# Moving one PSUM copy ahead of an exponent in the activation engine's order (pooling and state-space decoder trunk)

## The chip, the cores and the metric

The kernel runs on one core of one Trainium2 chip. The metric is the device time in microseconds of one execution. Engines: PE is TensorE, with PEld its weight loads; DVE is VectorE; ACT is ScalarE; POOL is GpSimd; SP is SyncE, which issues the DMAs.

## The reference

Two layers on 512 tokens of width 1024. Layer 0 mixes tokens by causal pooling, layer 1 by a Mamba-2 state-space mixer; each is followed by a squared-ReLU MLP of width 4096. The change lies in the state-space mixer, whose core, per group g of 8 heads and chunk c of 128 tokens, is:

```python
x, dtc, bc, cc = chunks of xs, dt, B, C
xdt = x * dtc[..., None]
a_cs = jnp.cumsum(adt, axis=-1)
seg = a_cs[..., :, None] - a_cs[..., None, :]
decay = jnp.exp(jnp.where(causal, seg, -jnp.inf))
cb = jnp.einsum("bclgn,bcsgn->bcgls", cc, bc)
y_diag = jnp.einsum("bcgls,bcgrls,bcsgrp->bclgrp", cb, decay, xdt)
decay_to_end = jnp.exp(a_cs[..., -1:] - a_cs)
states = jnp.einsum("bclgn,bcgrl,bclgrp->bcgrpn", bc, decay_to_end, xdt)
```

After it the output is gated by SiLU(z), and each group of 512 channels is divided by the root of its mean square (grouped RMSNorm) before the output projection.

## The kernel before, in words

Activations lie with features on partitions and the 512 tokens in the free dimension. Every weight product is done in three matmuls of rounded parts (line 710): a weight tile is rounded by ACT into `w_hi` (line 381), POOL subtracts it from the raw tile into `w_lo` (line 612), and TensorE multiplies high by high, high by low and low by high (lines 712 to 714). A unit is a 128-column slice of weights with 1024 rows, that is eight tiles and 24 matmuls; it is rounded and subtracted in two halves. Two units fit in the buffers, so ACT may round half h of unit u+2 once TensorE is done with half h of unit u (line 379), and POOL follows ACT (line 610). SP loads the raw weights once POOL has subtracted the unit two ahead (line 287).

The state-space mixer runs over groups g = 0 to 3. In each, every engine walks through the same slots t, one unit of the input projection per slot, with the scan's work laid into the slots by hand. All engines execute in the order in which their own loop is written, and semaphores join them. Around the change, in group g:

- TensorE (loop at line 912): after unit t=1 (`T_TOKEN`) `token_major` transposes B into a PSUM bank, `b_misc` (line 861), then takes C by B for all chunks (line 870) and transposes x for chunks 0 to 2 (line 852). After unit t=2 (`T_LATE_TOKEN`) it transposes x of chunk 3 into that same bank, so it waits for `bt_ready`, the copy's semaphore (line 926). After unit t=3, from group 1 on, it waits for the three square sums of the previous group (`ysum`, line 930) and runs `statistic_by_token`, eight recorded matmuls of one column (line 739). Then comes `chunk(g, 0)`: sixteen recorded matmuls of 64 x 128 (line 893), and the state product of the B copy and `decayed` x (lines 906 to 910), which waits for POOL.
- ACT (loop at line 563): each slot rounds one half (`ahead(u, 0)`), does some work, and rounds the other (`ahead(u, 1)`). Slot 1 then has the four squares of the previous group (line 554) and `exp_segments(g, 0)`: eight Relus of 128 x 128 (line 546) and an Exp of 128 x 1024 (line 549). Slot 2 is `ahead(u, 0)`, `b_token(g)` (the copy of the transposed B out of PSUM, line 537), `ahead(u, 1)`, `exp_segments(g, 1)`.
- POOL (loop at line 690): slot 2 is the subtraction of the first half, from group 1 on the three sums of squares (`group_sum`, line 684), the subtraction of the second half, and `decayed` of chunks 0 and 1 (line 671).
- DVE (loop at line 1265): slot 2 is C by B under the mask, x times dt for chunks 0 to 2 (line 1172), the scaling of the unit's output (`gate_in`, line 1245), and `decay_times_cb(g, 0)`, the product of the exponent and the masked C by B (line 1182). Slot 3 begins with x times dt of chunk 3.

The tables that place the work by slot:

```python
CHUNK_AFTER = {3: 0, 5: 1, 7: 2, 9: 3}
FALL_IN = {1: 0, 2: 1, 4: 2, 6: 3}
T_TOKEN, T_LATE_TOKEN = 1, 2
T_STAT, T_SPREAD = 3, 6
```

Of the kernel before, what the change touches and what calls it, by code (L numbers as in the profile page):

```python
# [56 lines left out]
T_TOKEN, T_LATE_TOKEN = 1, 2  # L57
# [5 lines left out]
def slot_of(g, t):  # L63

    return 7 + PER_GROUP * g + t
# [8 lines left out]
def slots(g):  # L74

    return PER_GROUP if g < GROUPS - 1 else GT + 16
# [7 lines left out]
def build(nc, xt, x_tok, pooling, weights, params, consts, out_t):  # L84
    ctx = ExitStack()
    with ctx:
# [280 lines left out]
        def _(act):  # L367
# [23 lines left out]
            def prepare(n, m, slot, last=False):  # L391


                if slot is not None:
                    act.wait_ge(ssq_added, add_base[n] + m - 1)
                s, count = prep_from[n] if n > 1 else (acc_drained, 0) if m < 2 else (pool_added, -2)
                act.wait_ge(s, count + m + 1)
                if last and isinstance(m, int) and m == KD - 1:
                    square(m, slot)
                if last:  # L400
                    act.activation(hg[:, bass.ds(m, 1), :], h[:, bass.ds(m, 1), :], ACT.Copy,
                                   scale=col(gains[n], m)).then_inc(hg_ready, 1)
                else:
                    act.activation(xhi[:, bass.ds(m, 1), :], h[:, bass.ds(m, 1), :], ACT.Copy,
                                   scale=col(gains[n], m)).then_inc(xhi_ready, 1)
                if slot is not None and not (last and isinstance(m, int) and m == KD - 1):
                    square(m, slot)

            def root(k, buf=r_tok):
                act.wait_ge(stat_drained, k + 1)  # L410
                act.activation(buf[:, :], buf[:, :], ACT.Sqrt).then_inc(sqrt_done, 1)
# [71 lines left out]
            def ahead(u, half):  # L483

                round_half(U_SSM + u + 2, half)

            def first_tap(n):

                act.wait_ge(scaled, n + 1)
                act.activation(conv_out(n), acc3[conv_slot(n) % 3][:, :], ACT.Identity,  # L490
                               scale=col("conv_w", 24 * (CONV_K - 1) + n), bias=col("conv_b", n)
                               ).then_inc(tap_ready, 1)
# [19 lines left out]
            def silu_b_c(g):  # L512

                for q in range(2):
                    act.wait_ge(acc_drained, A_SSM + conv_slot(CONVS * g + q) + 1)
                    act.activation(conv_out(CONVS * g + q), conv_out(CONVS * g + q), ACT.Silu).then_inc(bc_act, 1)

            def silu_x(g):
                act.wait_ge(acc_drained, A_SSM + conv_slot(CONVS * g + CONVS - 1) + 1)
                act.activation(xact[:, :, :], xact[:, :, :], ACT.Silu).then_inc(x_act, 1)  # L520

            def skip(g):

                act.wait_ge(x_act, g + 1)
                for i in range(GT):
                    act.activation(yx[:, GT * g + i, :], xact[:, i, :], ACT.Copy,  # L526
                                   scale=col("skip", GT * g + i)).then_inc(skip_ready, 1)

            def silu_z(g):

                act.wait_ge(acc_drained, A_SSM + slot_of(g, GT - 1) + 1)
                z = zs[:, GT * g:GT * g + GT, :]
                act.activation(z, z, ACT.Silu).then_inc(z_act, 1)

            def b_token(g):
                act.wait_ge(bt_mm, g + 1)
                act.activation(bt[:, :, :], b_misc[:, :].rearrange("p (c n) -> p c n", c=CHUNKS),
                               ACT.Copy).then_inc(bt_ready, 1)

            def exp_segments(g, c):  # L540

                act.wait_ge(m_landed[c % 2], 16 * (c // 2 + 1) + 32 * g)
                for h in range(HPG):
                    part = mbuf[:, c % 2, P * h:P * h + P]
                    at_head = HEADS * c + HPG * g + h
                    last = act.activation(part, part, ACT.Relu, scale=-1.0, bias=acs[:, at_head:at_head + 1])  # L546
                last.then_inc(fall_ready, 1)
                act.wait_ge(fall_ready, 4 * g + c + 1)
                act.activation(mbuf[:, c % 2, :], mbuf[:, c % 2, :], ACT.Exp, scale=-1.0).then_inc(exp_done, 1)

            def group_squares(g):
                for i in range(GT):
                    act.wait_ge(gated, GT * g + i + 1)
                    act.activation(sq[:, i, :], yx[:, GT * g + i, :], ACT.Square).then_inc(ysq_ready, 1)  # L554

            def norm_hi(g):

                for i in range(GT):
                    act.wait_ge(yn_ready, GT * g + i + 1)
                    act.activation(act_hi[:, GT * g + i, :], yx[:, GT * g + i, :], ACT.Copy,  # L560
                                   scale=col("norm_g", GT * g + i)).then_inc(yhi_ready, 1)

            for g in range(GROUPS):
                ends = g == GROUPS - 1
                for t in range(slots(g)):
                    u = slot_of(g, t)
                    ahead(u, 0)
                    if t == 0:
                        silu_b_c(g)
                        silu_x(g)  # L570
                        if g:
                            silu_z(g - 1)
                    if t == 2:
                        b_token(g)
                    if t == T_STAT + 1 and g:
                        root(SSM_STAT + g - 1)
                    if ends and t == T_STAT_END + 1:
                        root(SSM_STAT + g)
                    ahead(u, 1)
                    if not ends and t >= GT:  # L580
                        first_tap(CONVS * (g + 1) + t - GT)
                    if t == 0:
                        skip(g)
                    if t == 1 and g:
                        group_squares(g - 1)
                    if t in FALL_IN:
                        exp_segments(g, FALL_IN[t])
                    if t == T_SPREAD + 1 and g:
                        norm_hi(g - 1)
                    if ends and t == 8:  # L590
                        silu_z(g)
                    if ends and t == 10:
                        group_squares(g)
                    if ends and t == T_SPREAD_END:
                        norm_hi(g)
                    if ends and t >= T_OUT + 4:
                        prepare(3, 2 * (t - T_OUT - 4), None)
                        prepare(3, 2 * (t - T_OUT - 4) + 1, None)
# [816 lines left out]
```

## Time and profile before

| what | value |
|---|---|
| median of 3 runs | 1129.32 us (1129.31 to 1129.73) |
| the profiled execution | 1128.71 us |
| its span, first to last instruction | 1126.9 us |
| mean granted TensorE clock | 0.994 |
| PE busy | 1103.1 us (98%) |
| PEld busy | 903.6 us (80%) |
| DVE busy | 563.7 us (50%) |
| ACT busy | 462.8 us (41%) |
| POOL busy | 578.4 us (51%) |

Times in the rows are microseconds from the span's start. A timeline row is start, duration, engine, line, operation, what it writes and reads, and how many instructions it merges; in brackets stands how long the engine was idle ahead of it and what released it. A matmul's shown duration is longer than the distance to the next one, as they are pipelined, so distances of starts are used. A granted clock of 1.00 is 2.4 GHz, 0.50 is 1.2 GHz.

### The profile page before, as it was taken

To read this page: it belongs to the slowest core of one execution; us is meant where nothing else is said; L and a number is where in the kernel's file an instruction comes from. 1 tells how busy PE (TensorE), PEld (TensorE's weight loads), DVE (VectorE), ACT (ScalarE), POOL (GpSimd) and SP (SyncE) were. 2 spreads that over 40 slices of the span, in tenths; PEclk is the share of its full clock that TensorE was granted. 3 is DMA by queue.
4 is the path that set the end of the run, shared out by engine and by line. 5 is a ranking of instruction groups with operands and counts; after the bars stand their busy time and mean duration, and the time that the engine had idled before them with its cause. 6 is when DMAs were issued, how large, how long until landed. Compare 5 with 4: busy or idle time off the path is not lost.

```text
span 1126.9 us, 15338 instructions
## 1 busy us (share of the span) xinstructions
PE 1103.1 (98%) x5142; PEld 903.6 (80%) x5142; DVE 563.7 (50%) x663; ACT 462.8 (41%) x793; POOL 578.4 (51%) x440
## 2 busy tenths in 40 slices
PE   8999999999999999999999999999999999999996
PEld 6788888888888788787777877888888888888885
DVE  6655422455422473664857745566564224554213
ACT  7433222233333437566486675343332222333331
POOL 4666544445566545436344354546765444545551
PEclk9999999999999999999999999999999999999997
DMA  6332222233222234332423333223222223322222
GB/s 257 96 106 96 94 93 93 94 103 101 94 93 93 94 96 140 122 129 89 137 86 134 121 103 104 83 92 100 98 93 94 93 93 99 105 93 94 93 93 74
DMA packets 39428, 117.41 MB, mean 104 GB/s; under 512 B 4064, under 2 KB 10720, under 8 KB 39392
## 3 DMA queue, kind: packets, MB, share of 16 engines
q1 hardware_dynamic: 39104, 116.21, 31.2%
q10 hardware_dynamic: 288, 0.73, 0.2%
q8 instruction: 21, 0.34, 0.1%
q14 instruction: 15, 0.12, 0.0%
HBM read 114.70 MB, written 2.23 MB: 104 GB/s over the span
## 4 chain that ended last, share of the span: by engine, by line
PE 90%; ACT 5%; DVE 2%; issue 1%; DMA 0%; POOL 0%; DVEq 0%; ACTq 0%
PE bank L712 28%; PE bank L714 28%; PE bank L713 28%; PE bank L893 1%; PE bank L902 1%; PE bank L910 1%; ACT w_hi L381 1%; ACT y_accumulated L526 1%; ACT m L546 1%; PE bank L762 1%; ACT squares L554 1%; ACT x_conv L520 0%; DVE x_lo L972 0%; DMA x_token<-x_tok 0%; ACT x_hi L428 0%
## 5 line engine op out<-in xcount | busy, mean ns | idle before, releaser
L612 POOL TENSOR_TENSOR w_lo<-w_raw,w_hi 128x512 fp32r<-128x512 f32 x374 | 498.9, 1338 | 493.4 <-ACT w_hi L381 493.4
L381 ACT ACTIVATE w_hi<-w_raw 128x512 fp32r<-128x512 f32 x374 | 233.1, 627 | 445.0 <-PE bank L714 444.0
L712 PE MATMUL bank<-x_hi,w_hi 128*128 128x512 f32 x856 | 339.7, 397 | 2.8 <-DVE x_lo L972 1.7
L714 PE MATMUL bank<-x_hi,w_lo 128*128 128x512 f32 x856 | 333.3, 389 | 0.0
L713 PE MATMUL bank<-x_lo,w_hi 128*128 128x512 f32 x856 | 333.1, 389 | 0.0
L712 PE MATMUL bank<-act_hi,w_hi 128*128 128x512 f32 x640 | 252.1, 394 | 0.0
L714 PE MATMUL bank<-act_hi,w_lo 128*128 128x512 f32 x640 | 249.1, 389 | 0.0
L713 PE MATMUL bank<-act_lo,w_hi 128*128 128x512 f32 x640 | 249.0, 389 | 0.0
L712 PEld LDWEIGHTS bank<-x_hi,w_hi 128*128 128x128 f32 x856 | 160.7, 188 | 40.2 <-issue 6.0
L713 PEld LDWEIGHTS bank<-x_lo,w_hi 128*128 128x128 f32 x856 | 160.8, 188 | 35.2 <-issue 2.9
L714 PEld LDWEIGHTS bank<-x_hi,w_lo 128*128 128x128 f32 x856 | 160.7, 188 | 33.8
L1073 DVE TENSOR_TENSOR tmp<-bank,rstd 128x512 f32<-128x512 f32 x32 | 22.1, 692 | 240.5 <-PE bank L714 240.5
L713 PEld LDWEIGHTS bank<-act_lo,w_hi 128*128 128x128 f32 x640 | 120.2, 188 | 26.3 <-issue 1.7
L712 PEld LDWEIGHTS bank<-act_hi,w_hi 128*128 128x128 f32 x640 | 120.2, 188 | 26.3 <-issue 1.2
L714 PEld LDWEIGHTS bank<-act_hi,w_lo 128*128 128x128 f32 x640 | 120.1, 188 | 25.1
L1058 DVE TENSOR_TENSOR tmp<-tmp 128x512 f32<-128x512 f32 x64 | 116.1, 1814 | 2.2
L468 ACT ACTIVATE act_hi<-tmp 128x512 f32 x64 | 40.5, 632 | 122.1 <-DVE tmp L1058 122.1
L1055 DVE TENSOR_SCALAR tmp<-bank 128x512 f32<-128x512 f32 x64 | 44.3, 692 | 83.6 <-PE bank L714 83.6
L1062 DVE TENSOR_TENSOR act_lo<-tmp,act_hi 128x512 f32 x64 | 45.9, 717 | 59.0 <-ACT act_hi L468 59.0
L628 POOL TENSOR_TENSOR square_sum<-square_sum,squares 128x512 f32<-128x512 f32 x31 | 48.2, 1555 | 32.5 <-ACT squares L388 32.5
L1076 DVE TENSOR_TENSOR residual<-residual,tmp 128x512 f32 x32 | 53.5, 1673 | 4.9 <-DVE tmp L1073 2.5
L1101 DVE SCALAR_TENSOR_TENSOR x_conv<-bank,params,x_conv 128x511 f32<-128x511 f32 (+2 forms) x48 | 35.9, 749 | 15.2 <-ACT x_conv L490 14.0
(130 smaller groups left out, 654.2 us busy)
## 6 DMA issues: line engine op xcount, KB each, us to landing
w_raw<-weights SPq DMA_DIRECT2D x187, 512.0 KB, 3.3
m<-acs_scratch SPq DMA_DIRECT2D x16, 512.0 KB, 4.5
decay_in<-eacs_scratch SPq DMA_DIRECT2D x24, 128.0 KB, 3.7
x_token<-x_tok SPq DMA_DIRECT2D x4, 512.0 KB, 6.7
residual<-xt SPq DMA_DIRECT2D x8, 256.0 KB, 9.8
out_t<-scaled_residual SPq DMA_DIRECT2D x8, 256.0 KB, 2.4
pooling_matrices<-pooling ACTq DMA_DIRECT2D x1, 576.0 KB, 5.3
constants<-consts SPq DMA_DIRECT2D x1, 192.0 KB, 10.2
```

Source lines behind the costliest of these rows:

```text
L381: act.activation(whi[:, c % 2, part], raw[:, c % 2, part], ACT.Copy).then_inc(hi_ready, 1)
L468: act.activation(act_hi[:, bass.ds(2 * i + e, 1), :], tmp[:, e:e + 1, :], ACT.Copy).then_inc(hid_hi_ready, 1)
L612: pool.tensor_tensor(wlo[:, c % 2, part], raw[:, c % 2, part], whi_f[:, c % 2, part], ALU.subtract).then_inc(lo_ready, 1)
L628: pool.tensor_tensor(ssq[:, :], ssq[:, :], sq[:, slot, :], ALU.add).then_inc(ssq_added, 1)
L712: pe.matmul(out, wh, xh, start=start, stop=False)
L713: pe.matmul(out, wh, xl, start=False, stop=False)
L714: return pe.matmul(out, wl, xh, start=False, stop=stop)
L1055: dve.tensor_scalar(tmp[:, e, :], acc[(a - a0) % 2][:, :], 0.0, None, ALU.max).then_inc(acc_drained, 1)
L1058: dve.tensor_tensor(tmp[:, e, :], tmp[:, e, :], tmp[:, e, :], ALU.mult).then_inc(hid_sq_ready, 1)
L1062: dve.tensor_tensor(act_lo[:, tile, :], tmp[:, e:e + 1, :], act_hi_f[:, tile, :], ALU.subtract).then_inc(hid_lo_ready, 1)
L1076: dve.tensor_tensor(h[:, tile, :], h[:, tile, :], tmp[:, e:e + 1, :], ALU.add).then_inc(h_done, 1)
L1101: dve.scalar_tensor_tensor(out=out[:, back:], in0=p[:, 0:TOK - back], scalar=col("conv_w", 24 * k + n), in1=out[:, back:], op0=ALU.mult, o ...
```

## The change

In ACT's loop over the slots the call of `b_token(g)` is taken out of slot 2, where it stood between the two halves of weight rounding, and put into slot 1 (`T_TOKEN`), behind the squares of the previous group and ahead of `exp_segments(g, 0)`. Nothing else is changed, and no other engine's order.

```diff
@@ -570,8 +570,6 @@
                         silu_x(g)
                         if g:
                             silu_z(g - 1)
-                    if t == 2:
-                        b_token(g)
                     if t == T_STAT + 1 and g:
                         root(SSM_STAT + g - 1)
                     if ends and t == T_STAT_END + 1:
@@ -583,6 +581,8 @@
                         skip(g)
                     if t == 1 and g:
                         group_squares(g - 1)
+                    if t == T_TOKEN:
+                        b_token(g)
                     if t in FALL_IN:
                         exp_segments(g, FALL_IN[t])
                     if t == T_SPREAD + 1 and g:
```

## Rows read from the trace of the kernel before

**Rows 1.** The page, part 4: the chain that ended last, by engine.
```profile
PE 90%; ACT 5%; DVE 2%; issue 1%; DMA 0%; POOL 0%; DVEq 0%; ACTq 0%
```

**Rows 2.** The waits, whole span: us in total, times, longest.
```profile
PE bank L852 <- ACT b_token L537: 7.1, 3, 2.4
```

**Rows 3.** Timeline of TensorE, group 1, slots 1 to 3.
```profile
500.47 0.60 PE L861 MATMUL bank<-constants,b_feature 128*128 128x128 f32 x4
...
508.37 0.39 PE L714 MATMUL bank<-x_hi,w_lo 128*128 128x512 f32 x1
511.12 0.66 PE L852 MATMUL bank<-constants,x_conv 128*128 128x128 f32 x4 [2.37 <-ACT b_token L537]
511.54 0.48 PE L712 MATMUL bank<-x_hi,w_hi 128*128 128x512 f32 x1
...
517.10 0.95 PE L739 MATMUL bank<-constants,square_sum 128*128 128x1 f32 x8
517.98 1.09 PE L893 MATMUL bank<-m,x_dt 128*64 128x128 f32 x16
519.00 1.12 PE L910 MATMUL bank<-x_dt_decayed,b_token 128*128 128x512 f32 x2
```

**Rows 4.** Timeline of ACT, the same stretch.
```profile
505.26 2.44 ACT L546 ACTIVATE m<-m,cumulated 128x128 f32<-128x128 f32 x8
...
509.97 0.61 ACT L381 ACTIVATE w_hi<-w_raw 128x512 fp32r<-128x512 f32 x1
510.49 0.58 ACT L537 ACTIVATE b_token<-bank 128x512 f32<-128x512 f32 x1
510.97 0.62 ACT L381 ACTIVATE w_hi<-w_raw 128x512 fp32r<-128x512 f32 x1
```

**Rows 5.** Timeline of POOL, the same stretch.
```profile
510.66 1.82 POOL L612 TENSOR_TENSOR w_lo<-w_raw,w_hi 128x512 fp32r<-128x512 f32 x1 [5.27 <-ACT w_hi L381]
512.43 1.30 POOL L684 TENSOR_TENSOR square_sum<-squares 128x512 f32<-128x512 f32 x1
513.87 2.73 POOL L684 TENSOR_TENSOR square_sum<-square_sum,squares 128x512 f32<-128x512 f32 x2
516.56 1.28 POOL L612 TENSOR_TENSOR w_lo<-w_raw,w_hi 128x512 fp32r<-128x512 f32 x1
517.79 2.05 POOL L671 TENSOR_TENSOR x_dt_decayed<-x_dt,decay_to_end 128x512 f32<-128x512 f32 x2
```

**Rows 6.** Line 671, whole span: durations in ns, and who waited for it.
```profile
L671 POOL TENSOR_TENSOR x_dt_decayed<-x_dt,decay_to_end x12: 1038/1047/1053, 444.0 to 671.7; 128x512 f32<-128x512 f32 x12
...
  PEld bank L910: 0.5, 3
```

**Rows 7.** Timelines of ACT and of TensorE, group 0.
```profile
438.93 0.58 ACT L537 ACTIVATE b_token<-bank 128x512 f32<-128x512 f32 x1
...
440.85 0.60 PE L852 MATMUL bank<-constants,x_conv 128*128 128x128 f32 x4
```

**Rows 8.** Timeline of TensorE at the kernel's end.
```profile
1111.44 0.95 PE L946 MATMUL bank<-constants,square_sum 128*128 128x1 f32 x8
1113.95 1.67 PE L949 MATMUL bank<-constants,squares 128*128 128x1 f32 x8 [1.56 <-ACT squares L388]
```

**Rows 9.** Short stretches there: PE busy, granted clock, DMA share, GB/s.
```profile
1114.00:1114.20 0.20, 0.20 (x3) 1.00 0.00 0
1114.20:1114.40 0.20, 0.20 (x3) 0.52 0.00 0
```

**Rows 10.** Line 754 at the kernel's start: timeline, then durations in ns.
```profile
1.21 5.42 PE L754 MATMUL bank<-zeros 128*128 128x512 bf16 x16 [1.21 <-DVE zeros L1000]
...
L754 PE MATMUL bank<-zeros x16: 379/567/634, 1.2 to 6.3; 128*128 128x512 bf16 x16
```

**Rows 11.** Timeline of DVE, group 1.
```profile
510.10 1.23 DVE L1182 TENSOR_TENSOR m<-m,cb_masked 128x1024 f32<-128x1024 f32 x1 [0.61 <-ACT m L549]
...
517.29 0.69 DVE L1245 TENSOR_TENSOR z_silu<-bank,rstd 128x512 f32<-128x512 f32 x1 [4.79 <-PE bank L714]
```

## The prediction

> **What bounds the kernel now.** I read the chain of waits first: TensorE makes 90% of it [rows 1]. So a microsecond counts only where TensorE stands still, or where its clock falls. The wait list came next. In the state-space layer TensorE has one wait worth the name: three times, 7.1 us together, its transposes of line 852 wait for ACT's copy `b_token` [rows 2]. Then I read the four engines' timelines around one such place, group 1; the waits' counts of 3 say that groups 2 and 3 repeat it.
>
> TensorE ends unit t=2 at 508.60 (last matmul issued at 508.37, one every 0.23), waits, and starts the last transposes at 511.12, a stall of 2.5 us [rows 3]. ACT's order shows why: the eight Relus and the Exp of chunk 0 run from 505.26, the first half of the weight rounding at 509.97, and only then the copy at 510.49 [rows 4]. What the copy reads was ready early: the transposes of B began at 500.47 and took 0.6 [rows 3].
>
> The row to look at next is not TensorE's but POOL's. After that same rounding POOL runs without a gap: subtraction 510.66, three square sums from 512.43, subtraction 516.56, `decayed` of chunk 0 at 517.79, done 1.04 later at 518.83 [rows 5, 6]. Two TensorE steps need this chain: `statistic_by_token` after unit t=3 needs the three sums (done 516.60; TensorE came at 517.10, 0.5 later), and the state product of line 910 needs `decayed`. On the latter TensorE already waits, 0.5 us over three groups, 0.17 each [rows 6]. So two chains arrive nearly together, and the change shortens one.
>
> **The change, part by part.** (a) The copy moves ahead of the exponent of chunk 0. ACT reaches it at 505.26, when its input has lain there for over 4 us, so it adds no wait on ACT; `bt_ready` comes at about 505.8 instead of 511.07, and the stall at line 852 goes: TensorE does these transposes at 508.60. Gross gain 3 x 2.5 = 7.5 us. (b) Everything between the copy's new and old place comes later by what the copy takes of ACT: 510.97 - 510.49 = 0.48 us from its start to the next one's [rows 4]. That is the exponent of chunk 0 and the rounding of unit t=2's first half. From 510.97 on ACT is where it was. The exponent has cover: its product (DVE line 1182) would end near 511.8, and TensorE wants it at about 518. The rounding has none: POOL's chain hangs on it, and POOL executes in its written order, with the sums behind the subtraction. (c) So POOL's chain moves by +0.48: sums done at 517.08, `decayed` at 519.31. No part of it waits for TensorE, so the earlier transposes do not pull it forward.
>
> TensorE in the new order: transposes 508.60 to 509.02 (0.42, as from 511.12 to 511.54), unit t=3 of 5.56 us (511.54 to 517.10) to 514.58, then it waits for the sums until about 517.15: a stall of 2.6 us, the same stall in another place. Eight one-column matmuls of 0.88 and sixteen of chunk 0 (1.02) bring it to about 519.2; `decayed` ends at 519.31, and with the 0.17 from there to the start seen before, line 910 starts at 519.48 against 519.00 [rows 3, 5]. Net: +0.48 per group. Later waits start from the same point, and SP's weight loads, which stand behind POOL's subtractions, move with it. Group 0 has no square sums and no stall (copy at 438.93, transposes at 440.85, after the unit) [rows 7]: 0. No table load is added: the copy runs between squares and Relus, which load none. Sum of the order alone: 3 x 0.48 = +1.44 us.
>
> (d) **The clock.** Before, the 2.5 us stall lies between two units of dense 512-column matmuls, and the granted clock stays at 2.4 GHz. After, the stall is followed at once by the eight one-column matmuls, so that from 514.58 to about 518.2, 3.6 us, TensorE has no dense work, and then comes a chunk of half-width matmuls. The nearest row is the kernel's end: dense work stops at 1111.44, the same eight one-column matmuls follow, then a pause, and the granted clock falls to 1.2 GHz at about 1114.2, 2.8 us later [rows 8, 9]. The new light stretch is 0.8 us longer than that one; the old stall, 2.5 us, is shorter, and in three places the clock held. So a fall is likely in some of the three places, and I give each about one half. The Trainium skill, TensorE: Matmul & The Clock Gate ("What's actually happening"), says that recent activity sets this clock between the two levels, and that the moment differs between runs. By that the falls would differ from execution to execution.
>
> The price of a fall no row of this layer shows. From below it is 0 (a clock that returns at once, or falls within the wait for `decayed`); the nearest row is the start: sixteen 512-column matmuls began at 567 ns in the median, sped up to 379, and took 5.42 us where at the full rate (0.23 apart) they take 3.8 [rows 10]. So about 1.6 us is lost until the clock is back, once. From above I double it, since half-width work might not bring it back at once: 3.2. I take 1.6, as the work after is dense units like those. With one or two falls, 1.6 to 3.2, middle 2.4.
>
> The profiled execution took 1128.71 us, with 1126.9 of span. Against it: 1128.71 + 1.44 + 2.4 = 1132.6. The median of the runs is 1129.32, 0.61 above the profiled one, so I forecast 1129.32 + 3.8 = 1133.1. A measurement here tells 0.2%, 2.3 us, from no change.
>
> **The rivals.** *The order alone, clock held.* +1.44: 1130.8, not measurably slower. For it: the clock held over 2.5 us three times, and the half-width matmuls may count as work; against it: [rows 8, 9]. It decides from the first fall on: with one, +3.0, it is over the bound.
>
> *The gain arrives.* If the sums were ready before TensorE ends unit t=3, up to 7.5 us would go: 1121.8. That needs POOL's chain 2.5 us earlier, and it is released by ACT's rounding behind the exponent. A part is possible if POOL's subtraction runs at 1.29 instead of the 1.82 it takes beside DVE's product: 0.5 per group, which would only bring the sum to 0 (1129.3). But exponent, product and rounding shift together, so the overlap stays.
>
> *POOL slowed.* `gate_in` of unit t=3 on DVE (0.69) now falls at 514.6 into the middle of the sums. If it blocked POOL for its length, 3 x 0.69 = 2.1 more: 1132.9. Against it: at 517.29 the same instruction ran beside a subtraction of 1.28, which is as short as any [rows 5, 11]. The product of line 1182, with 0.67 us of overlap, does stretch POOL's subtraction to 1.82 [rows 5, 11]. The Trainium skill, GPSIMD Engine Reference ("Specifications"), says that DVE contends with POOL when it has two SBUF inputs; `gate_in` reads one from PSUM, so by that rule this rival adds 0, and the rows agree.
>
> *All three places fall, at up to the double price.* 1.44 + 3 x 1.6 = +6.2: 1135.6; at the double price it would be +11.0.
>
> **How the numbers follow.** Order plus one or two falls 0.48 (1132.4 to 1134.0 at 1.6 each); three falls, or dearer ones, 0.13; clock held 0.31; POOL slowed 0.03; a gain of any size 0.05. Of the last, most lies within 0.2%. Predicted: 1133.1. The range reaches down to the held clock with the runs' spread, 1130.3, and up to three falls, 1135.9. Own range of the likeliest case: 1131.9 to 1134.5. Faster by over 0.2%: 0.02; within: 0.34 (clock held, small gains, a cheap fall); slower: 0.64.
>
> **What the profile after would show.** Right: no wait of line 852 on line 537; `b_token` right behind the squares; POOL's subtraction near 511.1 in group 1; a TensorE wait of about 2.6 us ahead of line 739, released by line 684; line 910 starting about 0.5 later per group, still behind line 671; granted clock 0.5 for some microseconds after 517 in one or more of groups 1 to 3, with 512-column matmuls about twice as far apart as now. Wrong: group 2's copy-to-sum times not moved by 0.48 (the chain is not what I read); granted clock at 1.00 throughout with a time above 1131.6 (the loss lies elsewhere); or no wait at line 739.

## The result, and the profile after

The changed kernel takes 1137.72 us (median of 4, 1136.56 to 1137.88) against 1129.32 us before: a ratio of 1.0072, 95% interval 1.006 to 1.0084. It is 8.4 us slower; I had forecast 3.8 us slower, with a range that ended at 1135.9. The profiled execution took 1136.56 us, 7.85 above the one of before (1128.71), with a span of 1134.8.

The waits of the whole span in the changed kernel, us in total, times, longest:

```profile
DVE state L1189 <- PE bank L910: 11.9, 4, 3.7
DVE rstd_token L1225 <- PE bank L739: 10.1, 3, 3.6
...
PE bank L739 <- POOL square_sum L684: 7.5, 3, 2.5
```

The wait of line 852 on ACT's copy [rows 2] is gone, and in its place stands one of the same size, three times 2.5 us, 7.5 against 7.1 in sum: TensorE waits for POOL's square sums. The two DVE rows above it are new or larger (line 1189's was 7.1 before): what DVE gets from TensorE behind that wait comes late.

ACT's timeline in group 1, as [rows 4]:

```profile
503.26 2.18 ACT L554 ACTIVATE squares<-y_accumulated 128x512 f32<-128x512 f32 x4
505.34 0.58 ACT L537 ACTIVATE b_token<-bank 128x512 f32<-128x512 f32 x1
505.82 2.44 ACT L546 ACTIVATE m<-m,cumulated 128x128 f32<-128x128 f32 x8
508.28 1.28 ACT L549 ACT_TABLE_LOAD   x1
509.57 1.06 ACT L549 ACTIVATE m<-m 128x1024 f32<-128x1024 f32 x1
510.53 1.14 ACT L381 ACTIVATE w_hi<-w_raw 128x512 fp32r<-128x512 f32 x2
```

POOL's timeline there, as [rows 5]:

```profile
511.23 1.81 POOL L612 TENSOR_TENSOR w_lo<-w_raw,w_hi 128x512 fp32r<-128x512 f32 x1 [5.76 <-ACT w_hi L381]
513.00 1.28 POOL L684 TENSOR_TENSOR square_sum<-squares 128x512 f32<-128x512 f32 x1
514.43 2.68 POOL L684 TENSOR_TENSOR square_sum<-square_sum,squares 128x512 f32<-128x512 f32 x2
517.07 1.27 POOL L612 TENSOR_TENSOR w_lo<-w_raw,w_hi 128x512 fp32r<-128x512 f32 x1
518.30 2.05 POOL L671 TENSOR_TENSOR x_dt_decayed<-x_dt,decay_to_end 128x512 f32<-128x512 f32 x2
```

This execution lies 0.08 us later than the one of before as it comes into the group (squares end and next start at 505.34 against 505.26). Less that, the POOL rows stand 0.43 to 0.49 later than in [rows 5]: 511.23 against 510.66 (0.49), 518.30 against 517.79 (0.43).

TensorE's timeline there, as [rows 3]:

```profile
508.68 0.60 PE L852 MATMUL bank<-constants,x_conv 128*128 128x128 f32 x4
...
514.38 0.39 PE L714 MATMUL bank<-x_hi,w_lo 128*128 128x512 f32 x1
517.26 1.02 PE L739 MATMUL bank<-constants,square_sum 128*128 128x1 f32 x8 [2.49 <-POOL square_sum L684]
518.21 1.09 PE L893 MATMUL bank<-m,x_dt 128*64 128x128 f32 x16
519.39 2.08 PE L910 MATMUL bank<-x_dt_decayed,b_token 128*128 128x512 f32 x2
```

Line 910 starts at 519.39 against 519.00, but takes 2.08 instead of 1.12. The cause is in the clock. Stretches that hold the falls of groups 1, 2 and 3, with PE busy, granted clock, DMA share and GB/s:

```profile
518.00:524.00 6.00, 5.91 (x30) 0.72 0.32 93
...
591.00:598.00 7.00, 6.76 (x30) 0.51 0.27 83
...
666.00:673.00 7.00, 6.43 (x29) 0.51 0.22 75
```

In all three groups the granted clock fell to 1.2 GHz. The kernel before shows 1.00 in the same stretches, and around its own stall too, here that of group 3:

```profile
653.00:660.00 7.00, 4.78 (x23) 1.00 0.01 2
```

From the means, the time at half clock is (1 - 0.72) x 6 / 0.5 = 3.4 us in group 1, and 6.9 us in groups 2 and 3 (6.8 when it is added up from stretches of half a microsecond). In group 1 the fall came at 519.4, as line 910 began; in groups 2 and 3 it came at 591.06 and 666.15, before line 739 even started (591.24 and 666.57), and everything light ran at half clock too. The timeline of TensorE in group 2:

```profile
591.24 1.84 PE L739 MATMUL bank<-constants,square_sum 128*128 128x1 f32 x8 [2.50 <-POOL square_sum L684]
593.01 1.97 PE L893 MATMUL bank<-m,x_dt 128*64 128x128 f32 x16
594.91 2.08 PE L910 MATMUL bank<-x_dt_decayed,b_token 128*128 128x512 f32 x2
```

A ledger per group follows from POOL's first square sum, a place that every group has. Before: 512.43, 584.49, 656.53. After: 513.00, 586.99, 662.33. The lead grows from 0.57 to 2.50 to 5.80, so groups 1 and 2 cost 1.93 and 3.30. Each lead holds 0.49 of its own group's delay. From 5.80 less that 0.49 to 8.47 at line 946 (1119.91 against 1111.44), group 3 costs 3.16. The kernel's end, where the clock fell later this time, gives 0.6 back: 7.9 of span.

### The profile page after: what moved, and what is told of

The parts are those of the page before. It is cut to its first block, busy times and chain, and to the rows that moved or that the text cites. A ratio compares the mean times of both kernels' runs of the same rounds, so it can differ in the third digit from the quotient of the medians.

```text
span 1134.8 us, 15338 instructions
## 1 busy us (share of the span) xinstructions
PE 1110.1 (98%) x5142; PEld 908.1 (80%) x5142; DVE 561.7 (50%) x663; ACT 462.2 (41%) x793; POOL 577.7 (51%) x440
## 4 chain that ended last, share of the span: by engine, by line
PE 89%; ACT 4%; POOL 2%; issue 2%; DVE 2%; DMA 0%; DVEq 0%; POOLq 0%; ACTq 0%
PE bank L712 28%; PE bank L713 28%; PE bank L714 27%; PE bank L893 2%; POOL w_lo L612 1%; PE bank L910 1%; PE bank L902 1%; POOL square_sum L684 1%; ACT y_accumulated L526 1%; ACT w_hi L381 1%; PE bank L762 1%; ACT x_conv L520 0%; DVE x_lo L972 0%; DMA x_token<-x_tok 0%; ACT x_hi L428 0%
## 6 DMA issues: line engine op xcount, KB each, us to landing
constants<-consts SPq DMA_DIRECT2D x1, 192.0 KB, 10.2
```

## The experiments

**The changed kernel again** (no edit).

> The changed kernel once more, unaltered. Theory (order costs 0.48 us per group, and the granted clock falls to 1.2 GHz after the moved stall in groups 1 to 3, for 3.4 or 6.8 us each): about 1137 us, with three stretches at half clock whose lengths may differ from the first execution's 3.4, 6.8 and 6.8 us. Rival (one unlucky execution, or a cost that has nothing to do with the clock): fewer falls in the trace, and a time that does not follow their lengths.

Measured: 1136.86 us (1133.32 to 1137.8), ratio 1.0058 [1.0037, 1.0078]. Its profiled execution took 1137.80 us and fell three times, for longer in group 1 than the first. The stretches of group 1 in it:

```profile
514.00:518.00 4.00, 1.50 (x8) 0.90 0.00 0
518.00:524.00 6.00, 6.00 (x27) 0.50 0.32 96
```

The half-clock time is 0.8 + 6.0 = 6.8 us there, so 3.4 more than in the first execution, and the run is 1.24 us longer. The wait for the square sums is 7.5 us in both executions. So the time goes with the length of the falls, and these differ between executions: the four runs reach down to 1133.32. Of that run there is no trace, but its mean granted clock is 0.991, against 0.988 at 1136.01 and 0.986 at 1137.71 and 1137.80.

**Dense work in the moved stall.**

```diff
 if t == T_STAT and g:
     pe.wait_ge(cbm_ready, g + 1)
+    for _ in range(11):
+        pe.matmul(b_stat[:, :], xhi[:, 0, 0:P], xhi[:, 1, :], start=True, stop=True)
     pe.wait_ge(ysum, (GT - 1) * g)
```

> The changed kernel with eleven extra dense 512-column matmuls per group (1 to 3) in the moved stall, between unit t=3 and the wait for the square sums; they write a PSUM bank that is overwritten afterwards, about 2.5 us of work in a wait of 2.5 us. Theory (the clock is the larger part of the loss): no stretch at half clock inside the layer, the loss shrinks to the order's 3 x 0.48, so 1130.8 us (up to 1131.5 if the fill ends late). Rival (the loss is in waits and order alone): 1137.7 us, as the wait itself stays the same length.

Measured: 1128.75 us (1128.39 to 1129.68, 11 runs), ratio 0.9995 [0.9986, 1.0004]. TensorE in group 1, then the stretches of the three groups:

```profile
514.68 2.65 PE L931 MATMUL bank<-x_hi 128*128 128x512 f32 x11
517.28 1.05 PE L739 MATMUL bank<-constants,square_sum 128*128 128x1 f32 x8
518.27 1.09 PE L893 MATMUL bank<-m,x_dt 128*64 128x128 f32 x16
519.51 1.12 PE L910 MATMUL bank<-x_dt_decayed,b_token 128*128 128x512 f32 x2
```

```profile
514.00:524.00 10.00, 9.85 (x57) 1.00 0.18 55
588.00:598.00 10.00, 9.86 (x57) 1.00 0.30 105
662.00:672.00 10.00, 9.86 (x57) 1.00 0.46 157
```

Line 739 starts no earlier than in the changed kernel (517.28), so the wait for POOL is as long; only what TensorE does in it differs. With the clock held, 9.0 us of the changed kernel's 1137.72 are gone, more than the 8.4 it had lost, and the time is 2 us under the one expected; the last section says why. The clock is shown to be the larger part. The order alone is left: TensorE enters group 1 at 500.62 against 500.47 and starts line 946's counterpart at 1112.64 against 1111.44, so it lost 1.20 - 0.15 = 1.05 us over three groups, 0.35 each.

**Half as much of it**, in the same place:

```diff
-    for _ in range(11):
+    for _ in range(5):
```

> The changed kernel with five dense 512-column matmuls per group in the moved stall instead of eleven: 1.1 us of dense work, then about 1.4 us of stall, then the light matmuls. The light stretch is 2.4 us then, as long as the stall of the kernel before. Theory (the length of the light stretch decides): as the kernel before, none to two falls, 1128.7 to 1131.5 us. Rival (the wait right ahead of the one-column matmuls decides, whatever stands before it): 1135 to 1138 us.

Measured: 1130.49 us (1130.21 to 1132.24, 11 runs), ratio 1.0011 [1.0002, 1.002]. The profiled execution was the slowest of the eleven (1132.24) and shows two falls; four of the runs lie from 1131.7 to 1132.2 and seven from 1130.2 to 1130.6. These are the stretches of groups 1 to 3:

```profile
512.00:535.00 23.00, 21.71 (x117) 0.93 0.27 92
580.00:605.00 25.00, 23.57 (x112) 0.93 0.26 89
650.00:680.00 30.00, 28.55 (x156) 1.00 0.33 115
```

The wait stands ahead of the same light matmuls (1.29 us by the trace), and the loss is 1 us instead of 8. So a wait in that place is not enough for the large loss. The fill shortened the wait and with it the whole stretch without dense work, and this run alone does not tell the two apart; the eleven light calls below leave no wait, and the loss is there. In group 1 the fall began at 518.4, with the light work not yet done, and lasted 3.4 us.

**Light work in the stall.** First twenty-two calls of one column, ahead of the wait:

```diff
 if t == T_STAT and g:
     pe.wait_ge(cbm_ready, g + 1)
+    for _ in range(22):
+        pe.matmul(b_stat[:, 0:1], ident, ones[:, 0:1], start=True, stop=True)
```

> The changed kernel with the moved stall filled by twenty-two one-column matmuls (about 2.5 us) instead of dense ones; TensorE has an instruction running all the time, but next to no columns. Theory (light work counts as standing still): the clock falls as in the changed kernel, 1135 to 1138 us. Rival (any running matmul holds the clock): 1128.7 us as with the dense fill.

Measured: 1147.96 us (1145.91 to 1148.04), ratio 1.0155 [1.014, 1.0171]. As a test of the two theories it is spoiled by its size: each call became two instructions, and the fill took 6.3, 7.0 and 5.0 us in groups 1 to 3, partly at half clock, where the stalls were 2.5 each. That is 10.7 us more than the stalls, against 10.2 us more than the changed kernel. Half as many calls:

```diff
-    for _ in range(22):
+    for _ in range(11):
```

> The changed kernel with the moved stall filled by eleven one-column calls per group, which the trace of the run before shows as twenty-two instructions of 0.11 us, so about 2.5 us and no longer than the stall. Theory (one-column work counts as standing still): the clock falls in groups 1 to 3 as in the changed kernel, 1135 to 1138 us, although TensorE has an instruction running all the time. Rival (any running matmul holds the clock): 1128.7 us as with the dense fill.

Measured: 1136.65 us (1135.88 to 1137.71), ratio 1.006 [1.0044, 1.0075]. Its timeline of TensorE in group 1, and the clock by the microsecond:

```profile
514.51 2.51 PE L931 MATMUL bank<-constants 128*128 128x1 f32 x22
517.10 1.87 PE L739 MATMUL bank<-constants,square_sum 128*128 128x1 f32 x8
```

```profile
516.00:517.00 1.00, 1.00 (x10) 1.00 0.00 0
517.00:518.00 1.00, 0.92 (x6) 0.53 0.00 0
518.00:519.00 1.00, 1.00 (x7) 0.50 0.00 0
```

TensorE reads as busy all through, and the clock fell at about 517.1, as in group 1 of the changed kernel's second execution (517.2). One-column matmuls do here what standing still does.

**The square sums first.** What the moved stall waits for is freed from ACT's rounding, on top of the change:

```diff
-split_half(U_SSM + u + 2, 0)
 if t == 2 and g:
     group_sum(g - 1)
+split_half(U_SSM + u + 2, 0)
 split_half(U_SSM + u + 2, 1)
```

> The changed kernel, and POOL does the three square sums of slot 2 ahead of the first-half subtraction instead of behind it. Theory (the stall came back because POOL's sums hang on ACT's rounding): the sums are done near 509.5 in group 1, decayed x near 516.3, TensorE waits for neither, the clock holds, and the gross gain arrives: 1129.3 - 7.5 - 0.5 = 1121.3 us. Rival (a third chain stands close behind, such as the exponent's product or the second weight half): a new wait of 1 us or more per group, 1124 to 1130 us.

Measured: 1120.25 us (1119.86 to 1121.05), ratio 0.9921 [0.9907, 0.9934]: the gross gain of 7.5 us, and more. This version beats both kernels, by 9.0 us and 17.5 us. Its timelines of POOL and of TensorE in group 1:

```profile
505.69 1.31 POOL L684 TENSOR_TENSOR square_sum<-squares 128x512 f32<-128x512 f32 x1
507.14 2.72 POOL L684 TENSOR_TENSOR square_sum<-square_sum,squares 128x512 f32<-128x512 f32 x2
511.51 3.06 POOL L612 TENSOR_TENSOR w_lo<-w_raw,w_hi 128x512 fp32r<-128x512 f32 x2 [1.64 <-ACT w_hi L381]
514.52 2.04 POOL L671 TENSOR_TENSOR x_dt_decayed<-x_dt,decay_to_end 128x512 f32<-128x512 f32 x2
```

```profile
508.96 0.60 PE L852 MATMUL bank<-constants,x_conv 128*128 128x128 f32 x4
514.90 0.95 PE L739 MATMUL bank<-constants,square_sum 128*128 128x1 f32 x8
515.78 1.09 PE L893 MATMUL bank<-m,x_dt 128*64 128x128 f32 x16
516.80 1.12 PE L910 MATMUL bank<-x_dt_decayed,b_token 128*128 128x512 f32 x2
```

In the changed kernel POOL stood idle for 5.8 us ahead of 511.23; now the sums fill that hole, and TensorE waits neither at 852 nor at 739.

**The square sums first, without the change** (the same edit on the kernel before).

> The kernel before with only POOL's reordering: the three square sums ahead of the first-half subtraction. Theory (two chains arrive together, either alone gives nothing): the stall for the copy of B stays, only the 0.17 us wait of line 910 goes in three groups: 1128.8 us. Rival (the POOL order alone is what counts): 1122 us.

Measured: 1129.23 us (1127.87 to 1129.81, 11 runs), ratio 0.9996 [0.9987, 1.0005]. The wait stays as it was, and nothing of the 0.5 us came that I had put down to line 910: it starts 1.02 us behind line 893, as before (518.08, 519.10).

```profile
PE bank L852 <- ACT b_token L537: 7.1, 3, 2.4
```

So POOL's reordering alone changes nothing, this move of the copy alone loses 8.4 us, and both together gain 9.0: for the gain both orders had to change at once.

**The copy behind the exponent.** Slot 1 runs `exp_segments(g, 0)` first and `b_token(g)` after it:

```diff
-if t == T_TOKEN:
-    b_token(g)
 if t in FALL_IN:
     exp_segments(g, FALL_IN[t])
+if t == T_TOKEN:
+    b_token(g)
```

> The copy is in slot 1 as in the change, but behind the exponent of chunk 0 instead of ahead of it. POOL's chain is then pushed as in the change, while TensorE's stall is split: about 2.0 us at line 852 and 0.6 us at line 739. Theory (order costs 0.35 to 0.48 us per group, the rest of the loss is the clock falling behind a stall that runs into light work): no long fall, 1127.8 + 1.1 to 1.4 = 1128.9 to 1129.2 us, with no run above 1131. Rival (what costs is any stall at line 739 together with the light matmuls behind it): 1133 us or more, with falls in groups 1 to 3.

Measured: 1128.34 us (1127.53 to 1129.12, 11 runs), ratio 0.9987 [0.9978, 0.9996]. There is no fall inside the layer in the trace. The stall at line 852 is 1.85 us, and the one that I expected at line 739 is not there:

```profile
510.59 0.66 PE L852 MATMUL bank<-constants,x_conv 128*128 128x128 f32 x4 [1.85 <-ACT b_token L537]
516.72 1.02 PE L739 MATMUL bank<-constants,square_sum 128*128 128x1 f32 x8
```

```profile
511.13 1.32 POOL L612 TENSOR_TENSOR w_lo<-w_raw,w_hi 128x512 fp32r<-128x512 f32 x1 [5.76 <-ACT w_hi L381]
512.41 1.29 POOL L684 TENSOR_TENSOR square_sum<-squares 128x512 f32<-128x512 f32 x1
```

Here the copy stands between the exponent and the rounding, so DVE's product (510.08, 1.22 long) is nearly done when POOL's subtraction starts at 511.13. It takes 1.32 us, not the 1.82 of [rows 5], and POOL's sums start where they did before. The 0.5 us that the copy costs is paid back by the overlap that is gone. As line 739 does not wait here, the run says nothing on the rival, which needed a stall there.

**Dense work in the stall of the kernel before.** The same kind of fill, ten matmuls, ahead of line 926's wait:

```diff
 if t == T_LATE_TOKEN:
+    if g:
+        pe.wait_ge(cbm_ready, g + 1)
+        for _ in range(10):
+            pe.matmul(b_stat[:, :], xhi[:, 0, 0:P], xhi[:, 1, :], start=True, stop=True)
     pe.wait_ge(bt_ready, g + 1)
```

> The kernel before with ten dense 512-column matmuls per group (1 to 3) in its own stall ahead of line 852. Theory (the runs of the kernel before lie at 1127.8, 1129.3 and 1130.8 us because its stall, too, is followed by a short fall of the clock in none, one or two groups): the levels above 1128 go, all runs within 1127.7 to 1128.5 us. Rival (the levels come from something else, such as DMA or the start): the same three levels, median 1129.3 us.

Measured: 1127.79 us (1127.27 to 1128.49, 11 runs), ratio 0.9982 [0.9973, 0.9991]. The 21 runs of the kernel before beside it reach from 1128.13 to 1131.41. Line 852 starts at 511.17 in its group 1, against 511.12 in [rows 3], so the fill takes the place of the stall. Extra work makes the kernel 2 us shorter.

## Why the prediction was wrong

*The stall moves* (parts a to c): right, by its own numbers. The copy starts right behind the squares, `bt_ready` no longer holds TensorE, and the stall of 2.5 us came back as one of 2.5 us ahead of line 739, released by line 684. The run with the square sums first shows that this chain, and no third one, took the gain: 1120.25 us with the copy moved and the sums freed of the rounding, 1129.23 with the sums freed alone.

*+0.48 per group from the order*: right in kind, too large at the end. POOL moved by 0.43 to 0.49, but in the dense fill line 910 moved by 0.36 and TensorE by 0.35 per group, 1.05 in three groups and not 1.44. Before, line 910 began just as the chunk ahead of it ended (517.98 + 1.02 = 519.00), and the same 1.02 us stand there with the square sums first (515.78 to 516.80), where `decayed` was done over 1 us earlier. So the 0.17 us that I added as a wait behind `decayed` was not a wait on the path; with POOL truly last it is 0.06.

*The clock*: the mechanism was named, and it is what the dense fill shows; its size is the step that failed, twice: I took 2.4 us for it, and the runs showed 7.4, less 0.6 at the kernel's end. First the count: I gave each of the three places one half and took one or two falls; both traces of the changed kernel show three. The rows at the kernel's end had the clock fall 2.8 us after dense work ended. The new stretch of light work, which I put at 3.6 us, is 3.45 by my own figures (514.58 to 517.15 + 0.88), still beyond that; a half was too careful. Nor was 2.8 the least: in groups 2 and 3 the clock fell 2.5 and 2.2 us after the dense unit ended (588.59 and 663.93), while TensorE still waited.

Second the price: 1.6 us each, against 1.93 - 0.35 = 1.6 in group 1, 3.30 - 0.35 = 3.0 in group 2 and 3.16 - 0.35 = 2.8 in group 3. In group 2 `decayed` was done at 593.31 and line 910, slowed by the clock, started at 594.91 without waiting for it, so there the 0.35 overstates the order, and the clock's share lies between 3.0 and 3.3. The first, of 3.4 us at half clock, cost what I took; the two of 6.8 us cost near my upper bound of 3.2. Both began while TensorE still stood, so that all the light work that followed, statistic and chunk, ran at half clock before dense work came. Why these falls last twice as long is not shown. In group 1 the falls that began by 517.2 lasted 6.8 us (second execution, eleven light calls), and those that began at 518.4 and 519.4 lasted 3.4 (half the dense fill, first execution). That my 1.6 fits the shorter kind is in part luck: the sixteen matmuls of [rows 10] stood 0.42 us apart at first, as in a fall, but the profile grants them 1.00 and shows no fall there, and they could not tell how long one lasts in this layer.

The sum by what was measured: 1.05 + 1.6 + 3.0 + 2.8 = 8.45 us, less 0.6 at the kernel's end, against 7.85. It has to close, as the three prices are what the same trace leaves beside the order; that they are the clock's is what the dense fill shows. Of my own figures the rival of three falls at 1.6 each, +6.2, came nearest to the measured +8.4; it had 0.13 with the dearer falls. At the double price, +11.0, it lay nearer than my forecast too, and I left that out of the range.

The Trainium skill, TensorE: Matmul & The Clock Gate ("What's actually happening"), has the clock set by recent activity; the runs agree, with 9 us that come and go with what TensorE does in a wait of unchanged length.

*The rivals.* The order alone is refuted for the change, but is what the dense fill measures (1128.75). POOL slowed by `gate_in` is refuted: the sums took 2.68 us for two against 2.73 with `gate_in` among them. A subtraction at 1.29 was no part of this change, as argued, since exponent and rounding moved together; the copy behind the exponent, which parts them, shows that the effect is real (1.32 us).

## What to carry to other kernels

When a wait on TensorE is taken away, look for the next semaphore that the same slot needs, and ask which engine's order releases it: here the second chain had 0.5 us to spare, hung on the very engine whose order was changed, and was pushed by the move. If a stall has to be somewhere, put it between dense matmuls; in front of one-column and narrow ones it took the clock down and cost up to 3.0 us more than itself. And price a fall of the clock by all that runs while it lasts, here 3.4 or 6.8 us, not by the dense work alone.

## What I had not expected of the hardware

The kernel before holds falls too. Its runs lie in three bands: of the 21 beside the dense fill, six from 1127.8 to 1128.7, ten from 1129.2 to 1129.8 and five from 1130.8 to 1131.1, with mean granted clocks of 0.995 or 0.994, 0.994 or 0.993, and 0.992. The profiled execution of before happened to have none, and no trace of that kernel with a fall was taken. One with a fall, behind the same stall, is the profiled execution of the square sums first without the change; this is its stretch in group 3:

```profile
656.60:660.10 3.50, 3.50 (x10) 0.51 0.32 94
```

So the stall of 2.4 us between dense units does take the clock down at times, for 3.4 us; the distance of the bands, some 1.5 us, is then the price of one. With the stall filled (1127.79) or shortened to 1.85 us (1128.34) no run is above 1129.2. I had read three places without a fall, in one execution, as a clock that holds. It also accounts for the two runs that came out better than expected. With the square sums first the gain was counted from 1129.3, a median that holds a fall by this reading, while 7.5 us taken from the lowest band, 1127.8, gives 1120.3. And the dense fill, at 1128.75, is 0.9 us above the middle of that band (1127.9), near the 1.05 of the order.
